# A four-layer hybrid encoder step on one core: gate and pieces of the gated layers rearranged, start and end re-cut, a short first output block in the recurrent layer

## The chip, the core and the metric

The kernel runs on one core of a Trainium2 chip. The metric is the device time in microseconds of one execution, taken as the median of several runs. The engines are TensorE (PE, its weight loads PEld), VectorE (DVE), ScalarE (ACT), GpSimd (POOL) and the queue that issues most transfers (SP).

## What is computed

A streaming encoder step: 512 prompt tokens and 32 sample tokens of width 1024 go through four layers, whose mixers are gated linear attention (layers 0 and 3), banded attention (layer 1) and a gated linear recurrence (layer 2), each followed by a SwiGLU network, and a last normalisation:

```python
for i in range(4):
    x = x + mixer_i(rmsnorm(x, mix_norm_i))
    x = x + (silu(h @ w_g) * (h @ w_u)) @ w_out      # h = rmsnorm(x, ffn_norm_i)
y = rmsnorm(x, final_norm)

# gated mixer, per head: 128 keys, 256 values, chunks of 64 tokens
g = log_sigmoid((h @ w_gate_a) @ w_gate_b + b_gate) / 16      # w_gate_a: 1024 x 16
b = cumsum(g) within the chunk
a = where(causal, (q * exp(b)) @ (k * exp(-b)).T, 0)
o = a @ v + (q * exp(b)) @ S
S = exp(b_last) * S + (k * exp(b_last - b)).T @ v
y = (o * rsqrt(mean(o * o)) * head_norm * silu(r)) @ w_out
```

The recurrent mixer projects to two halves of 1536, runs a convolution of width 4, two block-diagonal gates and a scan over tokens, gates the result and projects it back. The states of the mixers are outputs too.

## The kernel before

The residual stream `x` stands in SBUF transposed, 8 tiles of 128 features by 544 tokens. Every projection is a list of blocks; a block makes 128 output features for all tokens. Its weights arrive in `raw[par]` (two buffers, taken in turn), ScalarE rounds them into `w_hi[par]` and VectorE subtracts into `w_lo[par]` (`split` in both engines' programs); the input is split the same way (`xg_hi`, `xg_lo`). For each input tile `k`, `k_step` makes three products (high by high, high by low, low by high), each as two matmuls of 272 columns into the PSUM tensor `slot[par]`. `mm_block` waits for the block's low weights (`s_lo`) and for its slot to be read (`s_free`). ScalarE's `split` of block b waits for block b-2 to be finished (`s_mm`), and SP's load of block b for the subtraction of block b-2 (`s_lo`).

Each engine has its own program, a list that is carried out strictly in order, with waits on semaphores. The mixers' other work is placed by hand between the k steps: `heads_at` gives, for a step number n, the heads under way and each one's own step, head h + 1 being 32 steps behind head h, and `head_step` in each engine's program says what is done at which of a head's steps. On TensorE these pieces are float32 matmuls and turns into the aux banks A0 to A3: `gate` (step 9), `turn_kd` (33), `scores` (34), `scores_sample` (36), `turn_v` (37, 39), `outer` for the sample (45) and for chunks 0 to 7 (46, 48, 50 in pairs, 52, 53), eight `out` pieces (54 to 61), `mean_sq` (66). VectorE's `cumsum` is at step 15, `q_decayed` at 20, `state` at 46 to 53; ScalarE's `decays` at 18; GpSimd's `keys` makes the two decayed key tiles of 544 tokens.

The first block of a gated layer is the low-rank product (`low_step`): 32 output rows, 16 from the rounded `w_gate_a` and 16 from its remainder. VectorE reads it as `GL["low"]` (32 rows), and `gate` multiplies it with two stacked copies of `w_gate_b` in float32.

At the start x arrives as rows, 128 tokens by 1024, in four transfers. TensorE runs warm-up matmuls on zeros, then turns the gain and the sample into bank A3, then the four row tiles, eight turns each, into the eight banks `X_BANKS`, the last of which is A3 too:

```python
for t in range(QT):
    pe.wait_ge(s_xr[t], 16)
    for m in range(XT):
        if t == 0 and m == XT - 1:
            pe.wait_ge(s_vc, 1)      # VectorE's copy of the gain out of A3
```

ScalarE meanwhile squares the rows in the order sample, 0, 1, 2, 3. ScalarE and VectorE then copy the banks to `x` and make `xg_hi` and `xg_lo`. The low-rank block runs as tiles become ready, then block 1.

In the recurrent layer four groups of three feature tiles are in work one behind the other; the last group is finished after the last input block, in `step` calls numbered from `XT * LRU_BLOCKS` on, and the output projection (12 input tiles per block) starts meanwhile, each k step waiting for its tile of `y_lo`. VectorE's `split` for the second output block stands between those steps, at `XT * LRU_BLOCKS + 7`, after the second tile's `y_lo` of the last group and before the third's.

At the end `last_project` adds the last blocks, ScalarE squares and scales x by the final gain (`xf`), TensorE turns it back into rows (`end_turn`); after the last block come the sum of squares, its mean over features on TensorE (`stat_sum`), the root, the inverse, the scaling of the rows in two halves of the features, and five output transfers.

## Time and profile before

| | |
|---|---|
| runs | 2732.36, 2733.41, 2733.16 us, median 2733.16 |
| profiled execution | 2730.5 us, of which the span from first to last instruction is 2728.8 |
| granted TensorE clock, mean | 0.997 |
| TensorE busy | 2700.2 us, 99% of the span |
| VectorE, ScalarE, GpSimd busy | 46%, 35%, 6% |
| read from HBM, written | 218.77 MB, 8.87 MB |
| warm-up matmuls | 1.68 to 8.8 us, row turns 9.48 to 13.2 us |

The busy time of TensorE is that of matmuls that overlap in the array; a line of the order of time gives start, duration from the first start to the last end, and the number of instructions merged. The distance from one start to the next says what an instruction costs.

### The profile page before, as it was taken

The numbers are of one execution on the slowest core, as the hardware profiler recorded it, in microseconds if no ns is written. First come the engines' busy times: TensorE is split into PE (matmuls) and PEld (weight loads), VectorE is DVE, ScalarE is ACT, GpSimd is POOL, SyncE is SP. The second block draws the span as 40 slices with busy tenths as digits, with TensorE's granted clock in tenths as the row PEclk, the third lists the DMA queues.
The fourth block names the chain that finished last, engine by engine and source line by source line (L and its number), as shares of the span: only waits on it lengthen the run. The fifth ranks groups of instructions, "written<-read, shape, count | busy, mean of one in ns | idle before, by whom it ended". The sixth has DMA issues, their size and how long they took to land.

```text
span 2728.8 us, 50596 instructions
## 1 busy us (share of the span) xinstructions
PE 2700.2 (99%) x21078; PEld 2604.4 (95%) x21078; DVE 1265.5 (46%) x1710; ACT 956.3 (35%) x1431; POOL 163.7 (6%) x172
## 2 busy tenths in 40 slices
PE   9999999999999999999999999999999999999998
PEld 8889999999988899999998899999999899999998
DVE  5565443344454554334456554434445555442442
ACT  5444322222454432222255632222224534221233
POOL 1101000001000010000112210000011101000001
PEclk9999999999999999999999999999999999999999
DMA  3222233232333222323322222332322123332332
GB/s 109 62 59 80 85 95 90 81 93 84 113 100 105 73 85 85 93 82 90 90 71 74 67 78 80 93 90 85 90 82 75 55 64 88 88 96 76 88 94 75
DMA packets 440699, 229.41 MB, mean 84 GB/s; under 512 B 15636, under 2 KB 436720, under 8 KB 440576
## 3 DMA queue, kind: packets, MB, share of 16 engines
q1 hardware_dynamic: 439328, 227.41, 28.7%
q8 instruction: 89, 1.46, 0.2%
q14 instruction: 34, 0.28, 0.0%
q0 software_dynamic: 192, 0.19, 0.0%
q10 hardware_dynamic: 1056, 0.07, 0.0%
HBM read 218.77 MB, written 8.87 MB: 83 GB/s over the span
## 4 chain that ended last, share of the span: by engine, by line
PE 94%; DVE 3%; issue 1%; ACT 1%; DVEq 0%; ACTq 0%
PE slot L1670 84%; PE aux L1632 2%; PE aux L2018 1%; PE aux L2014 1%; PE aux L1874 1%; PE aux L1815 1%; PE aux L1796 1%; PE aux L1928 1%; DVE w_lo L1063 1%; PE aux L1811 1%; DVE gla_s L1248 0%; DVE xg_lo L1075 0%; PE aux L1705 0%; DVE gla_b L1200 0%; PE aux L1761 0%
## 5 line engine op out<-in xcount | busy, mean ns | idle before, releaser
L1670 PE MATMUL slot<-xg_hi,w_hi 128*128 128x272 f32 x4352 | 926.1, 294 | 1.6 <-DVE w_lo L1063 1.5
L1670 PE MATMUL slot<-xg_hi,w_lo 128*128 128x272 f32 x4352 | 899.9, 288 | 0.0
L1670 PE MATMUL slot<-xg_lo,w_hi 128*128 128x272 f32 x4352 | 897.3, 288 | 0.0
L1670 PEld LDWEIGHTS slot<-xg_hi,w_hi 128*128 128x128 f32 x4352 | 681.4, 188 | 30.6 <-issue 24.4
L1670 PEld LDWEIGHTS slot<-xg_lo,w_hi 128*128 128x128 f32 x4352 | 683.7, 188 | 0.0
L1670 PEld LDWEIGHTS slot<-xg_hi,w_lo 128*128 128x128 f32 x4352 | 679.7, 189 | 0.0
L1063 DVE TENSOR_TENSOR w_lo<-raw,w_hi 128x1024 fp32r<-128x1024 f32 (+3 forms) x369 | 487.6, 1321 | 234.9 <-ACT w_hi L569 226.6
L569 ACT ACTIVATE w_hi<-raw 128x1024 fp32r<-128x1024 f32 (+3 forms) x369 | 410.2, 1112 | 358.0 <-PE slot L1670 347.0
L1670 PE MATMUL slot<-h_hi,w_hi 128*128 128x272 f32 x1408 | 290.8, 288 | 0.0
L1670 PE MATMUL slot<-h_hi,w_lo 128*128 128x272 f32 x1408 | 290.4, 287 | 0.0
L1670 PE MATMUL slot<-h_lo,w_hi 128*128 128x272 f32 x1408 | 290.4, 287 | 0.0
L1670 PEld LDWEIGHTS slot<-h_hi,w_hi 128*128 128x128 f32 x1408 | 220.0, 188 | 0.0
L1670 PEld LDWEIGHTS slot<-h_hi,w_lo 128*128 128x128 f32 x1408 | 220.0, 188 | 0.0
L1670 PEld LDWEIGHTS slot<-h_lo,w_hi 128*128 128x128 f32 x1408 | 219.9, 188 | 0.0
L1021 ACT ACTIVATE h_hi<-ffn_u 128x544 f32 (+1 forms) x88 | 58.0, 659 | 456.6 <-DVE ffn_u L1603 456.6
L1573 DVE TENSOR_TENSOR x<-slot,x 128x544 f32 (+1 forms) x80 | 57.9, 724 | 291.2 <-PE slot L1670 291.2
L2124 POOL TENSOR_TENSOR sq_sum<-sq_sum,sq_x 128x544 f32<-128x544 f32 x48 | 67.1, 1397 | 1806.4 <-ACT sq_x L587 1806.1
L1018 ACT ACTIVATE ffn_sg<-ffn_g 128x544 f32<-128x544 f32 x88 | 58.1, 660 | 316.6 <-DVE ffn_g L1081 316.6
L1081 DVE TENSOR_TENSOR ffn_u<-slot,rstd 128x544 f32<-128x544 f32 x88 | 63.7, 724 | 196.1 <-PE slot L1670 196.1
L1081 DVE TENSOR_TENSOR ffn_g<-slot,rstd 128x544 f32<-128x544 f32 x88 | 63.7, 724 | 132.5 <-PE slot L1670 132.4
L587 ACT ACTIVATE sq_x<-x 128x544 f32<-128x544 f32 (+1 forms) x56 | 36.8, 658 | 244.5 <-DVE x L1573 218.4
L1075 DVE SCALAR_TENSOR_TENSOR xg_lo<-x,vec_a,xg_hi (+1 forms) x64 | 70.8, 1112 | 68.4 <-ACT xg_hi L572 68.1
(285 smaller groups left out, 2354.4 us busy)
## 6 DMA issues: line engine op xcount, KB each, us to landing
raw<-in_l_ffn_w_in_dram SPq DMA_DIRECT2D x176, 512.0 KB, 3.8
raw<-in_l_ffn_w_out_dram SPq DMA_DIRECT2D x64, 704.0 KB, 4.5
raw<-in_l_gla_w_in_dram SPq DMA_DIRECT2D x48, 512.0 KB, 3.8
raw<-in_l_att_w_qkv_dram SPq DMA_DIRECT2D x24, 512.0 KB, 3.7
raw<-in_l_lru_w_in_dram SPq DMA_DIRECT2D x24, 512.0 KB, 3.8
raw<-in_l_gla_w_out_dram SPq DMA_DIRECT2D x16, 512.0 KB, 3.9
raw<-in_l_lru_w_out_dram SPq DMA_DIRECT2D x8, 768.0 KB, 4.7
att_bias<-bias_scratch SPq DMA_DIRECT2D x8, 512.0 KB, 4.1
```

The costliest lines, as they stand in the source:

```text
L569: act.activation(w_hi[par][:, 0:kt, :], raw[par][:, 0:kt, :], ACT.Copy).then_inc(s_hi, 1)
L587: act.activation(sq_x[par][:, :], one(x, m), ACT.Square).then_inc(s_xsq, 1)
L1018: act.activation(FF["sg"][:, :], FF["g"][:, :], ACT.Silu).then_inc(s_sg, 1)
L1021: act.activation(one(FF["h_hi"], t), FF["u"][:, :], ACT.Copy).then_inc(s_hhi, 1)
L1063: dve.tensor_tensor(w_lo[par][:, 0:kt, :], raw[par][:, 0:kt, :], w_hi[par][:, 0:kt, :].bitcast(F32), ALU.subtract).then_inc(s_lo, 1)
L1075: dve.scalar_tensor_tensor(one(xg_lo, m), one(x, m), gain(norm, m), one(xg_hi, m).bitcast(F32), ALU.mult, ALU.subtract).then_inc(s_xlo, 1)
L1081: dve.tensor_tensor(halves(dst), slot[par][0:rows, :, 0:HALF], halves(rstd[0:rows, :]), ALU.mult).then_inc(s_free, 1)
L1573: dve.tensor_tensor(halves(one(x, m)), slot[(p0 + j) % 2][:, :, 0:HALF], halves(one(x, m)), ALU.add).then_inc(s_free, 1)
L1632: return pe.transpose(out, in_, ident[rows, rows])
L1670: ins = pe.matmul(slot[par][:, hf, 0:HALF], w[par][:, k, :], a[:, k, hf * HALF:(hf + 1) * HALF], start=(k == 0 and at == 0), stop=(k == kt ...
L1796: pe.matmul(OUTER_BANK[c][:, 0:GLA_DV], GL["kd_t"][rows, c // 2, :], GL["v_t"][rows, c // 2, :], start=True, stop=True).then_inc(s_um, 1)
L2124: pool.tensor_tensor(sq_sum[:, :], sq_sum[:, :], sq_x[par][:, :], ALU.add).then_inc(s_xad, 1)
```

## The change

In the gated layers the low-rank product gets 96 rows: three times the rounded weights and three times their remainder, interleaved in pieces of 32. The product and `w_gate_b` (six stacked copies, loaded by GpSimd) are rounded by ScalarE, VectorE subtracts the remainders where a third needs them, and `gate` multiplies two tensors of the rounded format instead of float32 ones. TensorE's pieces are regrouped: `turn_kd` and `scores` at 34, `scores_sample` and the first `turn_v` at 37, the sample's outer product with chunks 0 and 1 at 46, chunks 6 and 7 together at 53, the output pieces in pairs at 55, 57, 59 and 61. `cumsum` moves from step 15 to 22, `decays` from 18 to 26, `q_decayed` from 20 to 28.

At the start the warm-up is 8 matmuls instead of 33, so the turns can begin when rows land. ScalarE splits the low-rank weights before the square of row tile 3; VectorE subtracts them as its first operation after the constants. ScalarE rounds block 1's weights in two halves and GpSimd subtracts them. ScalarE takes bank 6 over from VectorE. `first_pair` alternates the low-rank block and block 1 tile by tile, spreads the inverse before the last tile, and turns the vectors after it.

In the recurrent layer the output's first block takes only 9 of the 12 input tiles for output tile 0, the second is output tile 1, the third adds the 3 tiles left for output tile 0. The last block of the program is done for tokens 0 to 255 and then for the rest, and sum, root, inverse, turns, scaling and output follow for each part.

```diff
-WARM_UP = 23
+WARM_UP = 8
+LRU_OUT = [(0, 0, LT - GT), (1, 0, LT), (0, LT - GT, LT)] + [(m, 0, LT) for m in range(2, XT)]
+LRU_OUT_K = [k1 - k0 for _, k0, k1 in LRU_OUT]
...
-        X_BY_ACT = (3, 5, 7)
+        X_BY_ACT = (3, 5, 6, 7)
# ScalarE
             for n, t in enumerate((QT, *range(QT))):
+                if t == 3:
+                    split(0, 0, "low")
...
-                    if n == 18:
+                    if n == 26:
                         decays(h)
...
+                act.wait_ge(s_wb, 96 * (gl + 1))
+                act.activation(GL["wb"][:, :], GL["wb_in"], ACT.Copy).then_inc(s_wbh, 1)
                 split(b0 + 2, b0 % 2, XT)
+                act.wait_ge(s_free, b0 + 1)
+                act.activation(GL["low"][:, :], GL["low_in"], ACT.Copy).then_inc(s_lwh, 1)
...
# VectorE
+            split(0, 0, "low")
             dve.wait_ge(s_xt, 1)
...
-                    if n == 15:
+                    if n == 22:
                         cumsum(h)
-                    if n == 20:
+                    if n == 28:
                         q_decayed(h)
...
+                    stat_inv(0)
+                    gate_weights()
+                    dve.wait_ge(s_hi, 3)
+                    dve.wait_ge(s_wlo1, 2)
+                    dve.tensor_tensor(w_lo[0][:, 0:XT, :], raw[0][:, 0:XT, :], w_hi[0][:, 0:XT, :].bitcast(F32),
+                                      ALU.subtract).then_inc(s_lo, 2)
+                    stat_take(0, rstd)
+                    read(0, 0, GL["low_in"], GATE_ROWS)
+                    take_vectors()
+                dve.wait_ge(s_lwh, gl + 1)
+                dve.tensor_tensor(GL["low"][mid, :], GL["low_in"][mid, :], GL["low"][mid, :].bitcast(F32),
+                                  ALU.subtract).then_inc(s_lwl, 1)
...
                     if n == XT * LRU_BLOCKS + 7:
-                        split(b, b % 2, LT)
+                        split(b, b % 2, LRU_OUT_K[1])
# TensorE
             for n in range(WARM_UP):
                 pe.matmul(X_BANKS[n % 4][:, 0:HALF], w_lo[0][:, 0, :], zeros[:, 0:HALF], start=True, stop=True)
-            for n in range(6):
-                pe.matmul(X_BANKS[n % 4], w_lo[0][:, 0, :], zeros, start=True, stop=True)
-            for n in range(4):
-                pe.matmul(X_BANKS[n % 4][:, 0:P], w_lo[0][:, 0, :], zeros[:, 0:P], start=True, stop=True)
...
+            def first_pair(b0):
+
+                pe.wait_ge(s_lo, 1)
+                pe.wait_ge(s_x0, 2)
+                for k in range(XT):
+                    pe.wait_ge(s_xlo, k + 1)
+                    ins = low_step(b0 % 2, k)
+                    if k == XT - 1:
+                        ins.then_inc(s_mm, 1)
+                        pe.wait_ge(s_x0a, len(X_BY_ACT))
+                        stat_spread(0)
+                    if k == 1:
+                        pe.wait_ge(s_wlo1, 1)
+                        pe.wait_ge(s_x0, 3)
+                        pe.wait_ge(s_x0a, 1)
+                        k_step((b0 + 1) % 2, 0, XT, xg_hi, xg_lo)
+                    if k == XT // 2:
+                        pe.wait_ge(s_wlo1, 2)
+                    if 0 < k < XT - 1:
+                        k_step((b0 + 1) % 2, k, XT, xg_hi, xg_lo)
+                k_step((b0 + 1) % 2, XT - 1, XT, xg_hi, xg_lo).then_inc(s_mm, 1)
+                turn_vectors()
...
-                    if n == 33:
+                    if n == 34:
                         turn_kd(h)
-                    if n == 34:
                         scores(h)
-                    if n == 36:
+                    if n == 37:
                         scores_sample(h)
-                    if n in (37, 39):
-                        turn_v(h, (37, 39).index(n))
-                    if n == 45:
+                        turn_v(h, 0)
+                    if n == 39:
+                        turn_v(h, 1)
+                    if n == 46:
                         outer(h, NCHUNK)
-                    if n in (46, 48, 50):
-                        outer(h, n - 46)
-                        outer(h, n - 45)
-                    if n in (52, 53):
-                        outer(h, n - 46)
-                    if 54 <= n < 54 + VT * QT:
-                        out(h, (n - 54) // QT, (n - 54) % QT)
+                    if n in (46, 48, 50, 53):
+                        c = 2 * (46, 48, 50, 53).index(n)
+                        outer(h, c)
+                        outer(h, c + 1)
+                    if n in (55, 57, 59, 61):
+                        m = 2 * (55, 57, 59, 61).index(n)
+                        for at in (m, m + 1):
+                            out(h, at // QT, at % QT)
...
+                for c, (c0, tiles) in enumerate(END_PARTS[:2]):
+                    cols = slice(c0, END_PARTS[c + 1][0])
+                    for k in range(FH):
+                        for w, a, at in ((w_hi, FF["h_hi"], 0), (w_hi, FF["h_lo"], 1), (w_lo, FF["h_hi"], 2)):
+                            ins = pe.matmul(slot[par][:, c, 0:cols.stop - c0], w[par][:, k, :], a[:, k, cols],
+                                            start=(k == 0 and at == 0), stop=(k == FH - 1 and at == 2))
+                        if k == FH - 1:
+                            ins.then_inc(s_eh, 1)
+                        if c == 0 and k == 7:
+                            end_turn(XT - 2)
+                        if c and k == 4:
+                            end_sum(0)
+                        if c and k == 5:
+                            end_turn_last(0)
+                end_sum(1)
+                end_turn_last(1)
# GpSimd
+                if i == 0:
+                    pool.wait_ge(s_rsq, QT + 1)
+                else:
+                    pool.wait_ge(s_mm, b0)
-                for n in range(2):
-                    pool.dma_start(GL["wb"][n * GATE_RANK:(n + 1) * GATE_RANK, :], d[f"l{i}_gla_w_gate_b"]).then_inc(s_wb, 16)
+                for n in range(6):
+                    pool.dma_start(GL["wb_in"][n * GATE_RANK:(n + 1) * GATE_RANK, :], d[f"l{i}_gla_w_gate_b"]).then_inc(s_wb, 16)
```

## Rows read from the trace of the kernel before

**Rows 1.** The page, busy time of TensorE: us, share of the span, instructions.

```profile
PE 2700.2 (99%) x21078; PEld 2604.4 (95%) x21078; DVE 1265.5 (46%) x1710; ACT 956.3 (35%) x1431; POOL 163.7 (6%) x172
```

**Rows 2.** TensorE's waits: total us, times, longest us.

```profile
PE slot L1670 <- DVE lru_y_lo L1505: 3.8, 2, 3.2
PE aux L1796 <- DVE gla_s L1248: 3.0, 6, 0.5
```

**Rows 3.** TensorE around a gate, layer 0: start us, us, instruction, count.

```profile
60.22 0.41 PE L1670 MATMUL slot<-xg_lo,w_hi 128*128 128x272 f32 x2
60.47 0.41 PE L1670 MATMUL slot<-xg_hi,w_lo 128*128 128x272 f32 x2
...
61.92 0.52 PE L1670 MATMUL slot<-xg_hi,w_hi 128*128 128x272 f32 x2
62.28 0.41 PE L1670 MATMUL slot<-xg_lo,w_hi 128*128 128x272 f32 x2
```

**Rows 4.** TensorE at the outer products of a head.

```profile
66.70 0.70 PE L1796 MATMUL aux<-gla_v_t,gla_kd_t 64*128 64x256 f32 x4
...
73.35 0.41 PE L1670 MATMUL slot<-xg_hi,w_lo 128*128 128x272 f32 x2
73.69 0.70 PE L1796 MATMUL aux<-gla_v_t,gla_kd_t 64*128 64x256 f32 x2
74.31 0.52 PE L1670 MATMUL slot<-xg_hi,w_hi 128*128 128x272 f32 x2
...
75.83 0.48 PE L1796 MATMUL aux<-gla_v_t,gla_kd_t 64*128 64x256 f32 x1 [0.50 <-DVE gla_s L1248]
```

**Rows 5.** TensorE at an output piece.

```profile
78.26 0.41 PE L1670 MATMUL slot<-xg_hi,w_lo 128*128 128x272 f32 x2
78.51 0.38 PE L1811 MATMUL aux<-gla_at,gla_v_t 128*128 128x128 f32 x2
...
79.09 0.50 PE L1670 MATMUL slot<-xg_hi,w_hi 128*128 128x272 f32 x2
```

**Rows 6.** VectorE in the same stretch.

```profile
69.12 1.29 DVE L1200 TENSOR_TENSOR_SCAN gla_b<-chunk_go,gla_mn 128x544 f32<-128x544 f32 x1
...
74.73 1.05 DVE L1248 SCALAR_TENSOR_TENSOR gla_s<-gla_s,gla_dec,aux 128x256 f32<-128x256 f32 x2
```

**Rows 7.** The start in order of time, all engines.

```profile
1.68 5.42 PE L1637 MATMUL slot<-w_lo 128*128 128x272 f32 x23 [1.68 <-DVE w_lo L1045]
...
8.52 1.06 ACT L598 ACTIVATE x_rows_sq<-x_rows 128x1024 f32<-128x1024 f32 x1 [0.44 <-DMA x_rows<-in_x_prompt_dram]
...
12.16 0.60 PE L1632 MATMUL slot<-ident,x_rows 128*128 128x128 f32 x4
...
12.47 1.29 DVE L1100 COPY x<-slot 128x512 f32<-128x512 f32 x2 [2.39 <-PE slot L1632]
...
12.60 0.60 PE L1632 MATMUL aux<-ident,x_rows 128*128 128x128 f32 x4
...
32.57 0.72 PE L1741 MATMUL aux<-gla_low,gla_wb 32*128 32x272 f32 x2
```

**Rows 8.** TensorE and VectorE at the recurrent layer's first output blocks.

```profile
1580.22 0.78 PE L1670 MATMUL slot<-lru_y_hi,w_hi 128*128 128x272 f32 x2 [3.15 <-DVE lru_y_lo L1505]
...
1580.09 1.75 DVE L1063 TENSOR_TENSOR w_lo<-raw,w_hi 128x1536 fp32r<-128x1536 f32 x1
...
1594.75 0.72 DVE L1573 TENSOR_TENSOR x<-slot,x 128x544 f32<-128x544 f32 x1 [5.24 <-PE slot L1670]
```

**Rows 9.** A stretch there: length, PE busy, granted clock, DMA share, GB/s.

```profile
1583.50:1586.50 3.00, 3.00 (x15) 0.50 0.84 243
```

**Rows 10.** The end in order of time.

```profile
2715.00 0.41 PE L1670 MATMUL slot<-h_hi,w_lo 128*128 128x272 f32 x2
...
2719.58 2.46 DVE L1621 TENSOR_SCALAR end_rows<-end_rows,inv 128x512 f32<-128x512 f32 x6
```

**Rows 11.** A half microsecond of the outputs' transfer: length, clock, DMA share, GB/s.

```profile
2724.00:2724.50 0.50, 0.50 1.03 381
```

303 lines of the change are left out of this document (198 added, 105 removed).

## The prediction

> **What bounds the kernel now.** I read the page's first part first: TensorE is busy for 2700 of 2729 us [rows 1]. Then the waits of TensorE: everything it ever waits for on other engines is under 20 us, and the two largest pieces that this change aims at are the recurrent layer's last outputs and one state update in the gated layers [rows 2]. So the time is the length of TensorE's instruction list; a saving is either work taken off that list, or one of the few holes at the start, in the recurrent layer and at the end. Next I read TensorE's order of time, and priced every interruption of the stream of block matmuls. Two matmuls of 272 columns start 0.25 us after the two before them. An interruption costs the start of the next pair, less the start of the last pair, less 0.25, and then some 0.10 because the first pair after it is followed after 0.35 instead of 0.25 [rows 3].
>
> **Gate.** The gate's two float32 matmuls cost 61.92 - 60.47 - 0.25 + 0.10 = 1.30 us [rows 3], once for each of 8 heads (4 in each gated layer). Three stacked pieces in the block matmuls' own format are two matmuls of that format: 0.25, with the 0.10 of a change of stream 0.35. It saves 0.95; if the 96 rows kept all the extra of a 32-row matmul (about 0.3) 0.6, if they are as smooth as a block matmul 1.05. Eight times: 7.6 us (4.8 to 8.4).
>
> **Outer products.** Chunk 6 alone costs 74.31 - 73.35 - 0.25 + 0.10 = 0.81, and two chunks in the two halves of the rows take no longer (the group of four instructions lasts 0.70 like the group of two) [rows 4]. So chunks 6 and 7 in one go save one interruption: 8 x 0.81 = 6.5. Chunk 7 also stood 0.50 us for a state in six of the heads, 3.0 in all [rows 2, 4]. That state is late because VectorE does the next head's difference, scan (1.29, at 69.12) and two subtractions ahead of states 2 and 3, and so gets to 4 and 5 at 74.73 [rows 6]. The change puts them seven steps later, behind the last states. By the lengths of the steps states 4 and 5 are then done some 1.2 us before chunk 7 asks, though chunk 7 comes 0.81 sooner. I take the 3.0 whole (bounds 0 and 3.0). The sample's product joining chunks 0 and 1 saves an exit of 0.10 and an entry of 0.09 (0.34 from last pair to product [rows 4], against 0.25): 1.5 over the heads (0.8 to 3).
> A drain of the array would take part of that back: the Trainium skill, "TensorEngine Tiling (Array Packing)", Key Properties, says that a change of tiling mode drains TensorE, and here 32 rows are followed by 64. Rows 4 show 0.62 us for a product whose 4 x 256 columns, at 544 in 0.25, would fill 0.47, so the trace does not contradict it; by the rule the sum is nearer to 0.8 than to 1.5 for this term.
>
> **The rest of the pieces.** An output piece starts 0.25 after the last pair as any matmul would, so its overhead is the 0.10 at its exit [rows 5]. Eight output interruptions become four, and two more disappear (turned keys with scores, sample scores with the first turned value): 6 x 0.09 x 8 = 4.3 (0 to 4.8). Nothing in the work itself shrinks. Sum for the two gated layers: 7.6 + 6.5 + 3.0 + 1.5 + 4.3 = 22.9 us (12 to 26).
>
> What could be late next: the decay exponentials start at step 26 instead of 18, the turned keys at 34. For a head in the middle, ScalarE reads the previous head's first outputs (1.2), loads a table and takes the exponentials, then GpSimd makes both key tiles (one of them 2.3): by these lengths the second is done about 2.4 us before TensorE's step 34; for the first head of a layer, where no other pieces lengthen the steps, only 0.3 before. So zero, with little cover in two of the eight heads. ScalarE's and VectorE's two new conversions of gate weights and the low-rank product, and GpSimd's six loads instead of two (some 3 us of issuing instead of 1), lie in layer 3 under the second block, about 2.5 us clear of the first gate.
>
> **Start.** The long warm-up stood on TensorE until 8.8 us and the row turning ran from 9.5. Without it turning could follow the rows, but there is a wait: the last column tile of the first rows may not be turned until VectorE has taken the sample and the gain out of that bank. VectorE now first makes the low half of the low-rank weights, and that waits for ScalarE, which does its part only after the square of the third row tile: 8.52 + 1.06 + 0.19 = 9.8 us [rows 7]. Add that ScalarE copy (384 columns where the square's 1024 take 1.06, so about 0.5), VectorE's half 0.5, two copies 0.6: TensorE goes on at 11.4, with 25 of 32 turns still to do. Four turns start 0.44 after the four before, 0.11 each, at full rate [rows 7]. But the first 23 matmuls of the program took 5.42 us, 0.23 each, twice their later 0.125, until the array had been busy some 5 us [rows 7]. After 8 matmuls, a few turns and a hole to 11.4 it is slow again, I expect: 0.22 each. The first complete bank, after 18 turns, is ready at 13.4 (fast) or 15.3 (slow), where it was 12.47 [rows 7]: 0.9 to 2.8 us later.
> What wins it back: the second block runs inside the first, and its weight subtraction moves from VectorE to GpSimd. From the first copy to the second tile's remainder takes 3.7 as now: 19.0. From there 28 low-rank and 48 block matmuls at 0.125 and 1.05 for spreading the inverse: 29.5. The third block's weights need the low-rank block finished (27.7), then 1.06 and 1.2: 30.0, about with the end of turning the vectors. VectorE then copies the spread inverse (0.85), reads the low-rank product (0.68), takes the vectors (0.6), and with ScalarE's copy (0.66) makes the lower piece (0.68): 33.0. TensorE would have reached the gate at 31.5 and stands 1.5; it began at 32.57 [rows 7]. So the start loses 0.5 us; with turning at full rate it gains 1.4, with a longer slow stretch it loses 2.
>
> **Recurrent output.** TensorE stands 3.15 us for the tenth and eleventh remainder and then runs at half rate: granted clock 0.50, the 1.2 GHz level, to about 1587 [rows 2, 8, 9]. The short first block (9 tiles) ends at about 1576.2 without waiting. But the next block wants its low weights, and VectorE subtracts them only in the midst of the last group, at 1580.09, done 1581.84 [rows 8]. The order there is untouched; ScalarE's and VectorE's shorter split of the 9 tiles may bring it forward 0.5. So the wait is not removed, it changes its cause and grows: 1576.2 to about 1581.3. From there 12 tiles of 0.75 are 9.0, and a slow stretch as now costs 1.5 to 3.1, say 2.3: 1592.6. The remaining 3 tiles are 2.2, too short to cover ScalarE's 1.47 and VectorE's 1.76 for the next 12: another 1.0 of standing. 1595.9 against 1594.7, where VectorE's addition shows the second block over [rows 8]: a loss of 1.2 us (-0.5 to 2.5).
>
> **End.** The last block matmul ends at 2715.4, scaling begins at 2719.58, and the output's 2.23 MB flow at some 380 GB/s (5.9 us) until 1.0 us before the span's end: 13.4 us in all [rows 10, 11]. In two token parts the first 256 tokens are stored before the last matmul ends. After it, addition, square, sum (each about 0.25 shorter for 288 columns), six mean matmuls instead of ten (0.5 less) bring scaling to 2.9; VectorE needs 0.9 for the third tile of rows, and 1.18 MB at 380 GB/s are 3.1, with 0.8 before and 1.0 behind: 8.8. The first part's sum and turns now stand ahead of the last matmul, 0.8. Gain 13.4 - 8.8 - 0.8 = 3.8 us (2.5 to 4.6).
>
> **Sum.** -22.9 + 0.5 + 1.2 - 3.8 = -25.0. Against the profiled execution's 2730.5 that is 2705.5; the median of the runs shown is 2.7 above it, 2733.16, and gives 2708.2 us.
>
> **Rivals.**
> (a) The gated savings turn into waits: chunk 7's state still late (3.0 stays) and the keys late at step 34 in the heads, with the merged pieces saving nothing: 2708.2 + 3.0 + 4.3 + 2.5 = 2718. For it: 0.3 us of cover in each layer's first head, and VectorE and GpSimd ops that stretch beside each other (74.73 states wait behind a split) [rows 6]. Against: 2.4 in the middle heads.
> (b) My waits at the start and in the recurrent block are misread, so that both parts give what they are made for: start -3.0 instead of +0.5, recurrent -4.5 instead of +1.2: 2708.2 - 9.2 = 2699. For it: only orders of instructions speak for those waits, not rows. Against: each is a plain wait in a list read in order.
> (c) Slower than before: one mechanism, GpSimd's key tiles past step 34 in every head. To undo 25 us each of 8 heads must stand 3.1 us, so the tiles must come 5.5 later than worked out; at 4 us a head the time is 2740. Nothing in the rows is near it.
>
> **Chances and range.** Forecast 0.70, (a) 0.14, (b) 0.12, (c) 0.03, something near no change 0.01. The forecast's own range is 2701 to 2715 us; to leave no more than 2 in 10 out, 2699 to 2717. A change under 0.2% (5.5 us) can't be told from none here: faster 0.95, same 0.02, slower 0.03.
>
> **What would show it.** Gate interruptions of 0.35; no wait of an outer product for a state; four output interruptions a head; chunks 6 and 7 together in 0.8. TensorE idle from 7 to 11.4 us with the copy of the sample behind the low-rank subtraction, and a stand before the first gate. In the recurrent layer a wait of some 5 us for low weights after nine tiles. About 10 us from last block matmul to the span's end. A wait of the turned keys for GpSimd, or outer products still standing for states, would prove the sum wrong.

## Result, and the profile after

Four runs of the changed kernel took 2711.69 to 2713.05 us, median 2712.3; the kernel before, run beside it, 2732.8. The ratio is 0.9927, with a 95% interval of 0.9916 to 0.9939: 20 us faster. Forecast were 2708.2 us and a range of 2699 to 2717. The profiled execution took 2711.69 us, of which the span from first to last instruction is 2710.0; it is 18.8 us shorter than that of before, and 25.0 had been forecast.

Busy time of the engines on the page (it answers to [rows 1]), then the waits of TensorE (to [rows 2]: total us, times, longest):

```profile
PE 2679.9 (99%) x21037; PEld 2597.0 (96%) x21037; DVE 1264.9 (47%) x1717; ACT 958.9 (35%) x1440; POOL 166.1 (6%) x182
```

```profile
PE slot L1772 <- DVE w_lo L1118: 9.2, 5, 5.2
PE aux L1740 <- DVE vec_a L1159: 5.1, 1, 5.1
PE slot L1780 <- DVE xg_lo L1130: 2.6, 2, 1.7
PE slot L1772 <- DVE gla_sq L1136: 2.2, 1, 2.2
```

The waits of before are both gone: the outer products wait for no state, the recurrent output for no tile of y. Three have come: 5.1 us for the gain (`vec_a`), 5.2 of the 9.2 for low weights in the recurrent layer, and 2.2 for VectorE's read of the low-rank product, which nobody had forecast.

**Gated layers.** TensorE's order of time at a gate, an outer product of chunks 6 and 7, and an output piece of layer 0; they answer to [rows 3 to 5].

```profile
63.11 0.41 PE L1772 MATMUL slot<-xg_hi,w_lo 128*128 128x272 f32 x2
63.36 0.30 PE L1862 MATMUL aux<-gla_low,gla_wb 96*128 96x272 f32 x1
63.62 0.42 PE L1772 MATMUL slot<-xg_hi,w_hi 128*128 128x272 f32 x2
...
105.58 0.41 PE L1772 MATMUL slot<-xg_hi,w_lo 128*128 128x272 f32 x2
105.92 1.33 PE L1917 MATMUL aux<-gla_v_t,gla_kd_t 32*128 32x256 f32 x6
107.17 0.52 PE L1772 MATMUL slot<-xg_hi,w_hi 128*128 128x272 f32 x2
...
113.93 0.41 PE L1772 MATMUL slot<-xg_hi,w_lo 128*128 128x272 f32 x2
114.27 0.70 PE L1917 MATMUL aux<-gla_v_t,gla_kd_t 64*128 64x256 f32 x4
114.90 0.52 PE L1772 MATMUL slot<-xg_hi,w_hi 128*128 128x272 f32 x2
```

By the prediction's form (start of the next pair, less the last pair's, less 0.25, plus what the pair after is late) a gate costs 63.62 - 63.11 - 0.25 + 0.01 = 0.27 us (the pair after starts at 63.88) instead of 1.31. Chunks 6 and 7 together cost 114.90 - 113.93 - 0.25 + 0.11 = 0.83, what chunk 6 alone did. A whole gated layer is read from 0.25 us behind the start of the last pair ahead of its first gate to the start of the pair behind its last mean of squares. In layer 3, before and after:

```profile
2060.02 0.41 PE L1670 MATMUL slot<-xg_hi,w_lo 128*128 128x272 f32 x2
...
2243.10 0.50 PE L1670 MATMUL slot<-xg_hi,w_hi 128*128 128x272 f32 x2
```

```profile
2055.56 0.29 PE L1862 MATMUL aux<-gla_low,gla_wb 96*128 96x272 f32 x1
...
2228.14 0.50 PE L1772 MATMUL slot<-xg_hi,w_hi 128*128 128x272 f32 x2
```

That is 182.83 us before (from 2060.27) and 172.58 after, 10.25 less. Layer 0, read the same way, has 182.84 (32.48 to 215.32) and 172.75 (36.01 to 208.76), 10.09 less: 20.3 for the two.

**Start.** TensorE, then VectorE, in order of time; they answer to [rows 7].

```profile
11.87 0.47 PE L1740 MATMUL aux<-ident,x_rows 128*128 128x128 f32 x1 [5.13 <-DVE vec_a L1159]
12.13 1.06 PE L1740 MATMUL slot<-ident,x_rows 128*128 128x128 f32 x4
...
31.76 0.51 PE L1740 MATMUL aux<-ident,vec_rows 84*128 84x84 f32 x3
34.44 0.49 PE L1772 MATMUL slot<-xg_hi,w_hi 128*128 128x272 f32 x2 [2.17 <-DVE gla_sq L1136]
...
36.01 0.29 PE L1862 MATMUL aux<-gla_low,gla_wb 96*128 96x272 f32 x1
```

```profile
10.60 0.68 DVE L1115 TENSOR_TENSOR w_hi<-raw,w_hi 128x384 fp32r<-128x384 f32 x1 [8.10 <-ACT w_hi L589]
11.65 0.15 DVE L1159 COPY vec_a<-aux 128x8 f32<-128x8 f32 x1
16.00 1.29 DVE L1164 COPY x<-slot 128x512 f32<-128x512 f32 x2 [4.19 <-PE slot L1740]
```

The stand behind the gain copy is there as forecast, to 11.87 instead of 11.4; four turns then start 0.86 after the four before, 0.21 each. The first gate comes at 36.01 instead of 32.57 [rows 7]: 3.4 us lost where 0.5 had been forecast.

**Recurrent output.** TensorE, then VectorE; they answer to [rows 8].

```profile
1575.02 0.82 PE L1772 MATMUL slot<-lru_y_hi,w_hi 128*128 128x272 f32 x2 [5.22 <-DVE w_lo L1118]
1589.63 0.52 PE L1772 MATMUL slot<-lru_y_hi,w_hi 128*128 128x272 f32 x2 [1.06 <-DVE w_lo L1118]
```

```profile
1573.21 1.75 DVE L1118 TENSOR_TENSOR w_lo<-raw,w_hi 128x1536 fp32r<-128x1536 f32 x1
```

The nine-tile block runs through; the next one stands 5.22 us for low weights that VectorE subtracts at 1573.21, and behind the three-tile block come 1.06 more.

**End.** They answer to [rows 10].

```profile
2700.85 0.29 PE L2196 MATMUL slot<-h_hi,w_lo 128*128 128x288 f32 x1
2706.10 0.33 SPq L569 DMA_DIRECT2D out_dram<-end_rows  x1
```

The last matmul of the blocks ends at 2701.14, scaling begins 2.9 us later (2704.04), the last transfer is issued at 2706.10, and the span ends 8.8 us after that matmul instead of 13.4. No experiment takes this part of the change back alone; it is read from the two traces.

### The profile page after: what moved, and what is told of

Its sections match the earlier page's. It is cut to its first block, busy times and chain, and to the rows that moved or that the text cites. A ratio compares the mean times of both kernels' runs of the same rounds, so it can differ in the third digit from the quotient of the medians.

```text
span 2710.0 us, 50454 instructions
## 1 busy us (share of the span) xinstructions
PE 2679.9 (99%) x21037; PEld 2597.0 (96%) x21037; DVE 1264.9 (47%) x1717; ACT 958.9 (35%) x1440; POOL 166.1 (6%) x182
## 4 chain that ended last, share of the span: by engine, by line
PE 96%; DVE 2%; ACT 1%; issue 1%; DMA 0%; SPq 0%; DVEq 0%; ACTq 0%
PE slot L1772 85%; PE aux L1740 2%; PE aux L1917 1%; PE aux L2143 1%; PE aux L2139 1%; PE aux L1999 1%; PE aux L1936 1%; PE aux L2053 1%; PE aux L1932 1%; DVE w_lo L1118 1%; DVE xg_lo L1130 0%; PE slot L2196 0%; PE slot L1780 0%; PE aux L1882 0%; PE aux L1807 0%
## 5 line engine op out<-in xcount | busy, mean ns | idle before, releaser
L1118 DVE TENSOR_TENSOR w_lo<-raw,w_hi 128x1024 fp32r<-128x1024 f32 (+3 forms) x368 | 479.4, 1303 | 238.8 <-ACT w_hi L591 230.5
L591 ACT ACTIVATE w_hi<-raw 128x1024 fp32r<-128x1024 f32 (+4 forms) x369 | 409.3, 1109 | 359.3 <-PE slot L1772 345.7
L1692 DVE TENSOR_TENSOR x<-slot,x 128x544 f32 (+1 forms) x72 | 52.2, 725 | 261.3 <-PE slot L1772 261.3
L1130 DVE SCALAR_TENSOR_TENSOR xg_lo<-x,vec_a,xg_hi 128x544 fp32r<-128x544 f32 (+1 forms) x64 | 72.9, 1143 | 67.3 <-ACT xg_hi L594 67.2
```

Source lines behind the costliest of these rows:

```text
L591: act.activation(w_hi[par][:, 0:kt, :], raw[par][:, 0:kt, :], ACT.Copy).then_inc(s_hi, 1)
L1118: dve.tensor_tensor(w_lo[par][:, 0:kt, :], raw[par][:, 0:kt, :], w_hi[par][:, 0:kt, :].bitcast(F32), ALU.subtract).then_inc(s_lo, 1)
L1130: dve.scalar_tensor_tensor(one(xg_lo, m), one(x, m), gain(norm, m), one(xg_hi, m).bitcast(F32), ALU.mult, ALU.subtract).then_inc(s_xlo, 1)
L1692: dve.tensor_tensor(halves(one(x, m)), slot[(p0 + j) % 2][:, :, 0:HALF], halves(one(x, m)), ALU.add).then_inc(s_free, 1)
```

## Experiments

A time alone decides little here, because the start falls out differently from run to run (last experiment): the nine runs of the changed kernel lie between 2710.26 and 2714.85 us. So each trace is also read from one point behind the start, the gate of layer 0's second head, to the start of the last block matmul:

| kernel | median, us | second gate at | from it to the last matmul |
|---|---|---|---|
| changed | 2712.3 | 63.36 | 2637.49 |
| changed, again | 2712.07 | 66.30 | 2637.71 |
| VectorE's copies first | 2708.15 | 60.53 | 2637.45 |
| long warm-up | 2711.49 | 62.06 | 2638.16 |
| low-rank read first | 2711.29 | 63.42 | 2637.49 |
| recurrent split early | 2706.61 | 64.77 | 2630.39 |
| the three orders combined | 2701.63 | 60.72 | 2630.37 |
| the same, long warm-up | 2702.33 | 61.11 | 2630.42 |
| recurrent output as before | 2711.37 | 61.24 | 2635.40 |
| gate in float32 | 2718.04 | 61.75 | 2642.78 |
| outer products apart | 2720.65 | 61.88 | 2644.98 |
| scan as before | 2728.19 | 66.38 | 2650.93 |
| single output pieces | 2711.84 | 62.72 | 2637.56 |

**VectorE's copies first.**

```diff
-            split(0, 0, "low")
             dve.wait_ge(s_xt, 1)
             dve.tensor_copy(x[:, :, SEQ:TOK], ...).then_inc(s_xs, 1)
             dve.tensor_copy(vec_a[:, 0:XT], ...).then_inc(s_vc, 1)
+            split(0, 0, "low")
```

> VectorE copies the sample and the gain out of their bank before it subtracts the low-rank weights; nothing else differs from the changed kernel (2712.3 us). Theory (the start lost its time to TensorE's 5.1 us stand behind that copy, which waited in VectorE's list for ScalarE's third square): TensorE goes on turning within 1 us of its seventh turn, the first copy of x starts near 11.5 instead of 16.0 (now behind the subtraction alone), the first gate comes 3.5 to 4.7 us earlier; 2708.3 us. Rival (the start is set by the slow TensorE clock and by the work of ScalarE and VectorE on the tiles, so that turning earlier only moves the wait): the first gate moves by less than 1 us; 2711.5 us or more.

2708.15 us (ratio to before 0.9907, 0.9892 to 0.9922), 4.2 us less than the changed kernel; the theory had said 2708.3. (Between the two profiled executions, 2708.84 and 2711.69, it is 2.85.) The stand behind the gain is gone, the turns of the rows start at 5.72 us and run on, and the third block begins at 30.29:

```profile
30.29 0.79 PE L1772 MATMUL slot<-xg_hi,w_hi 128*128 128x272 f32 x2 [2.16 <-DVE gla_sq L1136]
30.88 0.65 PE L1772 MATMUL slot<-xg_lo,w_hi 128*128 128x272 f32 x2
```

The first copy of x starts at 11.55 instead of 16.00, 4.45 earlier. By the third block 4.15 are left (30.29 against 34.44), by the second gate 2.83: behind the stand of 2.16 two matmuls start 0.59 and then 0.45 after the two before, half rate, where the changed kernel's first trace went on at 0.32 and 0.25. So the wait costs the start; in this trace part of what its removal gives falls to the clock.

**Long warm-up.**

```diff
-WARM_UP = 8
+WARM_UP = 23      # and the ten longer warm-up matmuls of before behind them
```

> The changed kernel with the long warm-up of the kernel before (33 matmuls instead of 8), all else as changed. Theory (after the stand of 5.1 us the 25 turns ran at 0.21 each because TensorE had done too little): the long warm-up ends near 8.8, TensorE then stands only 1 to 2 us before the gain copy at 11.8, the turns run at 0.11 each, 2.5 us shorter in all, and the stretch at half rate near 20 us goes too, 1.1 more; 2709.5 us (3 us less). Rival (the clock falls in any case once TensorE waits for the tiles of x after 12 us): only the turns gain, or nothing; 2711 to 2712.5 us.

2711.49 us (2710.11 to 2713.99): by the time alone no difference that these runs can tell. The turns do run at 0.11 each and the first copy of x starts at 13.41, 2.6 earlier; the first gate is 2.5 earlier too (33.47). But a stretch at half rate comes behind the third block's stand (granted clock 0.50 from 30 to 34 us), and 1.2 us are lost again by the second gate:

```profile
30.62 0.79 PE L1776 MATMUL slot<-xg_hi,w_hi 128*128 128x272 f32 x2 [2.16 <-DVE gla_sq L1136]
31.21 0.66 PE L1776 MATMUL slot<-xg_lo,w_hi 128*128 128x272 f32 x2
```

Theory and rival are each half right: 1.3 us are left at the second gate. Behind it 0.67 more are lost, and 0.6 of them lie in the recurrent layer's output projection, which takes 81.09 us from its first to its last matmul instead of 80.47, though nothing in it was changed; it varies that much from trace to trace (see recurrent output as before).

**Low-rank read first.**

```diff
+                    stat_take(0, rstd)
+                    read(0, 0, GL["low_in"], GATE_ROWS)
                     dve.wait_ge(s_hi, 3)
                     dve.wait_ge(s_wlo1, 2)
                     dve.tensor_tensor(w_lo[0][:, 0:XT, :], ..., ALU.subtract).then_inc(s_lo, 2)
-                    stat_take(0, rstd)
-                    read(0, 0, GL["low_in"], GATE_ROWS)
```

> In layer 0 VectorE reads the low-rank product before it subtracts the third block's weights, instead of after; all else as changed (2712.3 us). Theory (the third block waits for its PSUM tensor, which the read frees, and the read stands in VectorE's list behind a subtraction that itself waits for ScalarE): the read fits into VectorE's idle time before 31.6 us, the third block starts when its weights are there, 32.85 instead of 34.44; the gate, whose inputs come earlier too, does not wait; 2710.7 us (1.6 us less). Rival (the subtraction is only pushed back by what the read takes, or the gate waits instead): 0 to 0.5 us less.

2711.29 us (2710.56 to 2714.34), and the second gate stands at 63.42, where it was. The third block does start earlier, at its weights, 33.01 instead of 34.44; but it then runs at half rate, and the 1.4 us are gone by the second gate:

```profile
33.01 0.63 PE L1772 MATMUL slot<-xg_hi,w_hi 128*128 128x272 f32 x2 [1.46 <-DVE w_lo L1379]
33.45 0.66 PE L1772 MATMUL slot<-xg_lo,w_hi 128*128 128x272 f32 x2
```

The theory had the mechanism and not its worth. The stand itself shrinks from 2.17 to 1.46 only, because the subtraction now stands behind the read: it starts at 31.75, 0.95 after ScalarE's rounding has ended, where the changed kernel had it 0.09 after (31.61). That the half rate comes of the edit is not shown: the changed kernel's second trace has it too, behind an unchanged stand (last experiment), and this trace has none at 20 us, where the first one had.

**Recurrent split early.**

```diff
-                    if n == XT * LRU_BLOCKS + 7:
+                    if n == XT * LRU_BLOCKS + 2:
                         split(b, b % 2, LRU_OUT_K[1])      # VectorE
```

> VectorE's subtraction for the recurrent layer's second output block moves five steps earlier (from step 7 to step 2 after the last input block); all else as changed (2712.3 us). Theory (the wait of 5.2 us for these low weights, and the half-rate stretch behind it, are the order of VectorE's list alone): both go, save some 1.75 us by which the tiles of y come later in that list and TensorE may wait for them; 2706.5 us (5.8 us less), no less than 3 us less. Rival (the same 1.75 us of VectorE stand in front of the last tiles of y, on which the nine-tile block waits, so the wait only moves from weights to tiles): within 1 us of 2712.3.

2706.61 us (ratio 0.9906, 0.989 to 0.9921), 5.7 less, and 7.1 between the two points of the trace: more than the theory said, because the later tiles of y cost only some 0.25 (a hole at 1571.05 in TensorE's order of time). The 5.22 us are gone from the waits, VectorE's subtraction starts 3.7 us earlier although this run's start was slower, and the remaining stand is the one behind the three tiles:

```profile
1569.51 1.73 DVE L1118 TENSOR_TENSOR w_lo<-raw,w_hi 128x1536 fp32r<-128x1536 f32 x1
```

```profile
1583.95 0.52 PE L1772 MATMUL slot<-lru_y_hi,w_hi 128*128 128x272 f32 x2 [1.06 <-DVE w_lo L1118]
```

**The three orders combined, and the same with the long warm-up.** Both are the diffs above put together.

> The three edits of VectorE's order together: sample and gain copied before the low-rank weights are subtracted, the low-rank product read before the third block's weights are subtracted, the recurrent layer's second output block split five steps earlier. Alone the first moved a later point of the start (the second head's gate) by 2.8 us, the second by nothing, because the clock fell to 0.50 behind the 1.5 us that TensorE still stood, the third took 7.1 us. Theory (the start's two stands each cost their length and a half-rate stretch behind them, so the second edit is worth something only when the first has taken the stand before the low-rank block's slow stretch away): the third block starts at its weights, some 0.6 us after the pair, with no half-rate stretch behind it; 2.8 + 7.1 + 2 to 3.5: 2699.5 us, at most 2701.5. Rival (the three only add up): 2712.3 - 9.9 = 2702.4 us or more.

> The same three edits with the long warm-up of the kernel before (TensorE then begins to turn rows at 8.4 us instead of 5). Theory (turning at once is worth more than turning fast, since the last rows land near 9 and VectorE is free only at 11.5): turns at 0.11 each from 9.1, the last banks near 12.7, the first copy of x at 11.6 or 12.4; within 1 us of the run with the short warm-up, and the low-rank block's first stretch at full clock where the short one showed 0.50 for 3 us: 2698 to 2700 us. Rival (the short warm-up is what makes the start short): 2 us longer than with it.

2701.63 us (2700.98 to 2702.16; ratio 0.9882, 0.9866 to 0.9898) and 2702.33 (2701.51 to 2702.62). The first is the fastest kernel of this study, 10.7 us below the changed one. It is the rival's sum (2702.4) rather than the theory's: the second gate stands at 60.72, no earlier than with the copies alone (60.53). The stand before the third block is 1.46, not 0.6: ScalarE may round its weights only when the low-rank block is finished (27.08 to 28.14), and VectorE subtracts them only behind the read, from 29.09 on (1.21). No half rate follows, and the first gate does come 1.2 us earlier than with the copies alone (31.97, 33.15). What takes this back is a new stand before the fifth block, which copies first does not have. ScalarE, then TensorE:

```profile
34.20 1.06 ACT L591 ACTIVATE w_hi<-raw 128x1024 fp32r<-128x1024 f32 x1 [4.33 <-DMA raw<-in_l_gla_w_in_dram]
```

```profile
44.23 0.52 PE L1772 MATMUL slot<-xg_hi,w_hi 128*128 128x272 f32 x2 [1.33 <-DVE w_lo L1118]
```

It goes back to a count. SP's load of the fourth block's weights needs only the second block's subtraction, which GpSimd now makes; but `s_lo` is raised for it only together with the third block's, by two. So the load goes out at 30.33 (at 32.87 in the changed kernel, at 20.98 before), and the read ahead of the subtraction makes it later still. The fourth block's rounding waits for it (34.20, above), VectorE's first work on the gate stands behind that block's subtraction, ScalarE's exponentials follow (from 37.37, where copies first has 35.80), and the fifth block's rounding stands behind these (41.87, 40.31). I ran no kernel with the count put right.

The long warm-up is 0.7 us behind the short one, within the 1 us of its theory, though both times lie some 2 us above what was expected. It doesn't keep the clock up either: the granted clock is 0.53 from 14 to 20 us with the short one, and 0.50 from 18 to 20 and again from 32 to 34 with the long one.

**Recurrent output as before.**

```diff
-LRU_OUT = [(0, 0, LT - GT), (1, 0, LT), (0, LT - GT, LT)] + [(m, 0, LT) for m in range(2, XT)]
+LRU_OUT = [(m, 0, LT) for m in range(XT)]      # with before's order of additions and splits
...
```

> The changed kernel with the recurrent layer's output projection as in the kernel before: eight blocks of twelve tiles, none split. Theory (the split first block gained nothing, since its wait for the tiles of y only became a longer wait for low weights, and one more stand of 1.06 us came behind the short third block; from the stretch's traces a loss of 1.7 us): 2710.6 us. Rival (the split block gained what it is for, 3 us, and the loss between the traces has another cause): 2715 us.

2711.37 us (2707.5 to 2712.79), by the time alone not to be told from the changed kernel; from the second gate to the last matmul 2635.40, 2.1 less. The waits are those of before again, 3.15 and 0.58. From its first to its last matmul the output projection takes 78.40 us here and 78.77 in the trace of before; in the nine traces that have it as changed it takes 80.06 to 81.09. So as the change was made, the short first block lost 1.3 to 2.7 us, 2.1 by this pair of traces.

**Gate in float32.**

```diff
-                    wb = GL["wb"][:, h * P:(h + 1) * P]
-                    pe.matmul(A2[:, 0:HALF], wb, GL["low"][:, 0:HALF], start=True, stop=True)
+                    wb, low = GL["wb"][:, h * P:(h + 1) * P].bitcast(F32), GL["low"].bitcast(F32)
+                    pe.matmul(A2[:, 0:HALF], wb, low[:, 0:HALF], start=True, stop=True)
...
```

> The changed kernel with the two gate matmuls in float32 on the same 96 rows; nothing else differs. The format's own cost: before, 32 rows in float32 made an interruption of 1.20 (by the trace, with its exit), after, 96 rows in the rounded format one of 0.26. Theory (the four passes of float32 are all of it; the number of rows costs nothing): 8 x 0.95 = 7.5 us more, 2719.8 us. Rival (part of the old cost was the change to 32 rows, which 96 rows avoid in any format): 4 to 6 us more, 2717.3 us.

2718.04 us (2715.39 to 2719.32), 5.7 to 6.0 more, and 5.1 to 5.3 between the two points. Up to 0.6 of these lie in the recurrent output projection (81.03 against 80.47 us), which this edit doesn't touch. TensorE's order of time at the gate itself:

```profile
61.49 0.41 PE L1772 MATMUL slot<-xg_hi,w_lo 128*128 128x272 f32 x2
61.75 0.62 PE L1862 MATMUL aux<-gla_low,gla_wb 96*128 96x272 f32 x2
62.21 0.62 PE L1863 MATMUL aux<-gla_low,gla_wb 96*128 96x272 f32 x2
62.46 0.61 PE L1772 MATMUL slot<-xg_hi,w_hi 128*128 128x272 f32 x2
```

The pair after starts at 62.91, so the gate costs 62.46 - 61.49 - 0.25 + 0.20 = 0.92 us, 0.65 more than the 0.27 of the changed kernel; the distance from the second gate to the third agrees (39.11 against 38.45). The rival is nearer, with 5.2 us for eight gates: of the 1.04 us that a gate got cheaper, some 0.65 are the format; the other 0.4 are the rows. With 32 rows the first matmul started 0.34 after the last pair, and the starts lay 0.57 and 0.54 apart (60.47, 60.81, 61.38, 61.92 in the trace of before [rows 3]); with 96 rows, in float32 as well, they are 0.26, 0.46 and 0.25.

**Outer products apart.**

```diff
-                    if n == 46:
+                    if n == 45:
                         outer(h, NCHUNK)
-                    if n in (46, 48, 50, 53):
-                        c = 2 * (46, 48, 50, 53).index(n)
+                    if n in (52, 53):
+                        outer(h, n - 46)
+                    if n in (46, 48, 50):
+                        c = n - 46
...
```

> The changed kernel with the outer products apart again: the sample's at step 45, chunk 6 at 52, chunk 7 at 53, chunks 0 to 5 in pairs. By the prediction's terms: 6.5 for chunks 6 and 7 (0.81 a head), 1.5 for the sample's product (0.8 by the Trainium skill's rule, "TensorEngine Tiling (Array Packing)", Key Properties, that a change of tiling mode drains TensorE), no wait for a state. Theory (a change of stream costs its drain each time, and two chunks in the two halves of the rows cost what one does): 0.72 to 0.81 a head for chunk 7, 0.10 for the sample: 6.5 + 0.8 = 7.3 us more, 2719.6 us. Rival (part of the gain came from the later scan alone, so that single chunks would wait for states too): with waits of 0.3 to 0.6 a head 2722 us or more.

2720.65 us (2717.71 to 2723.06); 7.3 to 7.5 us more between the two points (with a recurrent projection that is 0.4 shorter in this trace), and no outer product waits for a state. From a middle head's gate to its first output piece the trace has 101.33 to 117.02, 15.69 us, against 101.81 to 116.52, 14.71: 0.98 for a head, 0.8 of it chunk 7. The sample's product alone costs 105.30 - 104.34 - 0.25 + 0.11 = 0.82 and chunks 0 and 1 the same 0.83, together 1.65, against 107.17 - 105.58 - 0.25 + 0.11 = 1.45 in one go: 0.20 saved.

```profile
104.34 0.41 PE L1772 MATMUL slot<-xg_hi,w_lo 128*128 128x272 f32 x2
104.68 0.69 PE L1917 MATMUL aux<-gla_v_t,gla_kd_t 32*128 32x256 f32 x2
105.30 0.52 PE L1772 MATMUL slot<-xg_hi,w_hi 128*128 128x272 f32 x2
```

**Scan as before.**

```diff
-                    if n == 22:
+                    if n == 15:
                         cumsum(h)      # VectorE; decays 26 -> 18 on ScalarE, q_decayed 28 -> 20 on VectorE
```

> The changed kernel with the cumulative sum at step 15, the decay exponentials at 18 and the decayed queries at 20 of a head's steps again, with the merged pieces as changed. Theory (chunks 6 and 7 in one go ask for the states of 4 and 5 some 0.8 us sooner than chunk 7 did, so without the later scan the wait grows): a wait of 0.6 + 0.8 us in six of the eight heads, 8 us more, 2720.3 us, and in its trace outer products waiting for gla_s. Rival (the wait stays what it was, 3 to 3.4 us, since the two states are late by their own chain): 2715.5 us. Rival two (the merging itself made the later scan unnecessary): 2712.3 us.

2728.19 us (2726.27 to 2731.04): 16 of the change's 20 us are undone. Between the two points it is 13.2 to 13.4 us more, where the theory had said 8; the rest of the difference lies in the start, 1.0 of it a stand for the fifth block's low weights at 49.89. TensorE waits 7.3 us for states, six times. Its order of time at chunks 6 and 7:

```profile
118.66 0.70 PE L1917 MATMUL aux<-gla_v_t,gla_kd_t 64*128 64x256 f32 x2
120.84 0.70 PE L1917 MATMUL aux<-gla_v_t,gla_kd_t 64*128 64x256 f32 x2 [1.48 <-DVE gla_s L1309]
```

The wait of up to 1.48 us falls between the two chunks, so chunk 7 no longer runs in the other half of the rows beside chunk 6: each of the six heads pays the wait and the 0.7 of a chunk by itself. In two heads of each layer that is 2.17 (from first outer product to first output piece 12.77 against 10.60), in the first of each layer, with a wait of 0.7, it is 1.4: 11.5 for six. The rest of the 13.4 is no part of this: behind one of the waits, of 1.46 us in layer 3, the granted clock falls to 0.50, and the head takes 1.5 us longer than its like in layer 0:

```profile
2147.50:2150.80 3.30, 3.30 (x17) 3.30 (x16) 1.24 (x3) 0.90 (x1) 0.00 (x0) 0.50 0.32 96
```

Merging without the later scan would have been a loss of some 2 us: apart, with the waits of before, chunks 6 and 7 cost 6.4 + 3.0 = 9.4 more than in the changed kernel (worked out, not run), merged 11.5.

**Single output pieces.**

```diff
-                    if n in (55, 57, 59, 61):
-                        m = 2 * (55, 57, 59, 61).index(n)
-                        for at in (m, m + 1):
-                            out(h, at // QT, at % QT)
+                    if 54 <= n < 54 + VT * QT:
+                        out(h, (n - 54) // QT, (n - 54) % QT)
```

> The changed kernel with the eight output pieces of a head one to a step (54 to 61) instead of in pairs. By the prediction's step an interruption saved is worth 0.09 us: four a head, 8 x 4 x 0.09 = 2.9 us, 2715.2 us. Theory now (the trace of the changed kernel shows 1.26 for two pieces where one took 0.59: the 0.10 at the exit is there again between two pieces, so merging gives only 0.07 a head): 0.6 us more, 2712.9 us, no more than 1.

2711.84 us, and 2637.56 between the two points, 0.1 from the changed kernel. Pairing the output pieces is worth nothing. Alone, the first two pieces cost 115.48 - 114.87 - 0.25 + 0.08 = 0.44 and 116.90 - 116.07 - 0.25 + 0.09 = 0.67 in this trace, together 1.11; in the changed kernel's, below, the pair costs 117.55 - 116.26 - 0.25 + 0.08 = 1.12. What is saved at one exit is paid inside, where the first two matmuls of the second piece take 0.27 to the next start and those of the first 0.21.

```profile
116.52 0.38 PE L1932 MATMUL aux<-gla_at,gla_v_t 128*128 128x128 f32 x2
116.73 0.33 PE L1936 MATMUL aux<-gla_qe,gla_s 128*128 128x64 f32 x2
116.91 0.44 PE L1932 MATMUL aux<-gla_at,gla_v_t 128*128 128x128 f32 x2
117.18 0.56 PE L1936 MATMUL aux<-gla_qe,gla_s 128*128 128x64 f32 x4
117.55 0.49 PE L1772 MATMUL slot<-xg_hi,w_hi 128*128 128x272 f32 x2
```

**The changed kernel once more.**

> The changed kernel itself once more, for the measure of what another profile of the same program shows. Runs 2712.3 us. In an experiment that did not touch the start, its trace showed the second head's gate 1.4 us later than the first trace of the changed kernel, with a half-rate stretch behind the stand before the third block that the first trace did not have. Theory (the start falls out one way or another from run to run): this profile shows the gate at either 63.4 or 64.8 us, with or without that stretch. Rival (the first trace's start is the usual one): 63.4 within 0.2.

2712.07 us (2710.26 to 2714.85). The second gate stands at 66.30, beyond either value that the theory named. Six traces of programs with this start and gate show it between 61.24 and 66.30, a spread of 5 us:

| trace | first copy of x, us | second gate | between | granted clock, 0 to 60 us |
|---|---|---|---|---|
| recurrent output as before | 15.14 | 61.24 | 46.10 | 1.00 |
| outer products apart | 15.78 | 61.88 | 46.10 | 1.00 |
| single output pieces | 15.39 | 62.72 | 47.33 | 0.97 |
| changed | 16.00 | 63.36 | 47.36 | 0.97 |
| recurrent split early | 15.78 | 64.77 | 48.99 | 0.94 |
| changed, again | 16.14 | 66.30 | 50.16 | 0.91 |

Up to 1.0 us of the spread is there before the first copy; the other 4.1 go with the granted clock. Stretches of the start in recurrent output as before (earliest gate), changed (first trace), and changed again (latest gate); the clock is the third number from the end:

```profile
20.00:26.00 6.00, 6.00 (x51) 6.00 (x50) 5.20 (x7) 4.99 (x9) 3.23 (x7) 1.00 0.13 36
```

```profile
20.00:26.00 6.00, 5.87 (x37) 5.87 (x38) 4.90 (x7) 5.02 (x9) 4.09 (x7) 0.76 0.13 36
```

```profile
20.00:26.00 6.00, 5.74 (x25) 5.74 (x26) 4.91 (x7) 5.02 (x9) 4.22 (x7) 0.50 0.16 35
36.00:40.00 4.00, 3.97 (x19) 4.00 (x20) 2.84 (x8) 1.63 (x2) 0.00 (x0) 0.57 0.89 245
```

In 6 us TensorE gets through 51 records at full clock and 25 at the 1.2 GHz level. The stands ahead of these stretches are nearly the same in all three traces (4.9 to 5.1, 1.7 to 1.8, 0.9 and 2.2 us), so what made the clock differ is not shown. The Trainium skill, "TensorE: Matmul & The Clock Gate", Part 1, says that how many of a kernel's first matmuls run at the low clock varies from run to run; these traces agree, and show it 20 and 36 us into a kernel, behind stands of 0.9 to 2.2 us.

## Why the prediction was right, and which steps were off

The direction, the size within 4 us and the range were right, since two of the four parts came out within 0.5 us and a third, the gated layers, within 2.6 of 22.9. Against the profiled execution the miss is larger: 2705.5 forecast, 2711.69 measured, 6.2 us. The start is 2.9 of it, the gated sum 2.6, the recurrent part 0.5; 0.2 is not placed. On the medians 2.1 fewer are missing, and that is luck: the profiled execution of before lay 2.7 us under the median that the forecast was set on, that of after only 0.6 under its own.

- **Gate: right.** Forecast 7.6, measured 1.04 x 8 = 8.3. The upper of the two bounds held: 96 rows are as smooth as a block matmul. The gate in float32 shows that 0.4 of a gate's saving was the 32 rows.
- **Chunks 6 and 7, and the state wait: right.** 6.5 forecast; 0.8 a head measured, 6.4. The wait's 3.0 went whole. The forecast treated the two terms as independent; the scan as before shows that they are not, since a wait between the chunks costs the merging as well.
- **The sample's product: right at the row's value.** Forecast 1.5, measured 0.20 a head in the middle heads, 1.6 for eight. By the Trainium skill's rule on a drain at each change of tiling mode ("TensorEngine Tiling (Array Packing)", Key Properties) I had put it nearer to 0.8; the runs don't bear that out for this term, though the 0.4 of the 32-row gate and the 0.34 before a 32-row or 64-row product (0.25 before one of 128) are what such a drain would look like.
- **The rest of the pieces: mis-sized, and this is the gated sum's miss.** Forecast "6 x 0.09 x 8 = 4.3". 20.3 less the other terms (8.3, 6.4, 3.0 and 1.6) leaves 1.0, 3.3 short; the gate gave 0.7 of that back by being worth more than forecast. By the same form as above, in a middle head of both traces, the turned keys with the scores save 0.05 us and the sample's scores with the first turned value 0.06: 0.9 for eight heads, where the forecast had 1.4. The output pairs give nothing, where it had 2.9. The single output pieces show why: the exit of 0.10 that I took from [rows 5] is not a charge for an interruption that merging removes; between two merged pieces about the same is paid. For the outer products it did count, since there a whole second group ran in the time of the first.
- **Start: the step "TensorE would have reached the gate at 31.5 and stands 1.5" failed.** The forecast's list of what VectorE does before the read of the low-rank product was right, but I asked only when the gate could start, and not who else waits for that read: the third block uses the low-rank block's PSUM tensor, and stands 2.2 us for it before the gate is reached. The wait for the gain copy was right (forecast to 11.4, measured 11.87), and so were the turns at 0.22; the second tile's remainder came 1.1 later than forecast, and "a longer slow stretch" behind it (2.5 us at 0.50, 20.0 to 22.5) took the pair's end from 29.5 to 31.76. The loss of 3.4 us lies outside the term's bounds (-1.4 to 2), and other traces of the same start lose from 1.5 to 6.5 (second gate at 61.24 to 66.30, against 60.81 less the 1.04 of the first gate); of the start of before there is one trace only.
- **Recurrent output: right.** The wait (forecast some 5, measured 5.22), the second one (1.0 and 1.06) and the sign held. The loss is 1.7 us between the traces and 2.1 by experiment (1.3 to 2.7 over all traces), where 1.2 had been forecast. That the wait was the order of VectorE's list alone is shown by moving one call: 7.1 us.
- **End: right.** 8.8 forecast from last matmul to the end, 8.8 measured; with 0.7 ahead of it the gain is 3.8 us, as forecast. This rests on the two traces alone.

Of the rivals, (a)'s late keys and states did not come, though the merged pieces did save next to nothing, as it had them; (b), both waits misread, was wrong in the changed kernel, but its time (2699) is about what removing them gives: 2701.6 with both out of the way.

## What to carry to other kernels

When a block is moved forward, write down everything that its first instruction waits for (its weights, its PSUM buffer's last reader, its input) and where each stands in the other engine's list: all three stands of this kernel were an operation too late in VectorE's list, two of them behind one that itself waited, and moving one call took away 3 and 7 us at two of them. Ask the same of every count that is raised somewhere else than before: here a load of weights went out 12 us later for it, and TensorE only waited behind it once another edit had made that load later still. Merging small pieces pays where the second runs beside the first in the array or a stand disappears, and not by the number of interruptions; and two pieces run side by side only if both are ready. A stand of 1.5 to 2 us may cost some 1.5 us more through the clock, and in another run nothing more, so read such a change by two points of the trace and several traces of the same start before believing 1 or 2 us.

## What was not expected of the hardware

With the same start in the program, the second gate came up to 5 us apart from trace to trace, 4.1 of it by the granted clock: 1.00, 0.76 or 0.50 over the same 6 us, behind nearly the same stands. Behind the unchanged stand of 2.2 us before the third block the half rate came in the changed kernel's second trace and not in its first; so where it came with an edit (the read first, the long warm-up, where the third block began 1.43 and 3.8 us earlier and the second gate 0 and 1.3), the edit need not have caused it. Nor is it a matter of the start alone: in scan as before the clock fell to 0.50 at 2147 us, behind a wait of 1.46 us, and in the same trace did not fall behind waits of 1.48 us in layer 0.
